# Twelve chunks of ada_w in layer 0's qkv stage: multiplied and summed by partition on VectorE instead of on TensorE

## The reference, cut to what matters

```python
silu_c = jax.nn.silu(c)            # c: (1, 1024)
silu_cc = jax.nn.silu(c_ctx)       # c_ctx: (1024,)
for i in range(DEPTH):             # DEPTH = 2
    mod_l = (silu_c @ ada_w[i] + ada_b[i])[:, None, :]
    mod_c = (silu_cc @ ada_w[i] + ada_b[i])[None, None, :]
    sh1_l, sc1_l, g1_l, sh2_l, sc2_l, g2_l = jnp.split(mod_l, N_MOD, axis=-1)
    ...
    a_l = ada_norm(h, norm_mix[i], sh1_l, sc1_l)          # needs sh1, sc1
    y_l, y_c = neighbourhood_attention_mixer(a_l, a_c, na_w_qkv[slot], ...)
    h = h + g1_l * y_l                                    # needs g1
    h = h + g2_l * swiglu_ffn(ada_norm(h, norm_ffn[i], sh2_l, sc2_l), ...)
```

## Time and profile before

| quantity | value |
|---|---|
| median of three runs | 1595.96 us (1595.84 to 1598.35) |
| profiled execution, its own time | 1595.65 us |
| its span in the trace | 1594.3 us |
| mean granted TensorE clock | 0.995 of full |
| TensorE busy | 1553.4 us, 97% |
| VectorE busy | 909.5 us, 57% |
| ScalarE busy | 688.3 us, 43% |
| GpSimd busy | 67.3 us, 4% |
| data moved by DMA | 251.19 MB, 158 GB/s on average |

### The profile page before, as it was taken

One profiled execution on the slowest core, in us unless ns is written; L12 is line 12 of the kernel. 1 busy time (PEld: TensorE's weight loads), 2 busy tenths in 40 slices (PEclk: granted clock), 3 DMA queues, 4 the chain that ended last, 5 costly groups with the idle time before them and its releaser, 6 DMA issues.

```text
span 1594.3 us, 25726 instructions
## 1 busy us (share of the span) xinstructions
PE 1553.4 (97%) x11195; PEld 1381.7 (87%) x11195; DVE 909.5 (57%) x1184; ACT 688.3 (43%) x932; POOL 67.3 (4%) x92
## 2 busy tenths in 40 slices
PE   5999999999999999999999999999999999999998
PEld 4778866867888888878778999999999999999998
DVE  5322488453432443357866555568777655677763
ACT  4311487332312321235764444545545446554552
POOL 2010031000000000000000000034000000000000
PEclk8999999999999999999999999999999999999999
DMA  9764421745433222364134555565555555555551
GB/s 327 246 205 159 139 35 21 264 160 184 159 106 106 93 92 85 101 230 141 54 122 144 185 185 172 180 213 183 173 184 180 184 179 164 165 175 185 179 174 71
DMA packets 254240, 251.19 MB, mean 158 GB/s; under 512 B 17085, under 2 KB 252960, under 8 KB 254128
## 3 DMA queue, kind: packets, MB, share of 16 engines
q1 hardware_dynamic: 252880, 247.48, 48.0%
q0 software_dynamic: 928, 1.94, 0.3%
q10 hardware_dynamic: 320, 0.13, 0.0%
HBM read 248.49 MB, written 1.05 MB: 157 GB/s over the span
## 4 chain that ended last, share of the span: by engine, by line
PE 88%; DVE 4%; ACT 2%; POOL 2%; issue 1%; DMA 1%; SPq 1%; DVEq 0%; ACTq 0%; POOLq 0%
PE psum L362 86%; PE psum L869 2%; DMA pre<-in_ada_w 1%; DVE sums L932 1%; POOL ptmp L1766 1%; DVE pt L946 1%; ACT wh L341 1%; DVE wl L348 1%; SPq L290 0%; DMA raw<-in_ada_w 0%; POOL ptmp L1765 0%; ACT scr L899 0%; DVE acc L1545 0%; POOL scr L1773 0%; ACT xh L632 0%
## 5 line engine op out<-in xcount | busy, mean ns | idle before, releaser
L362 PE MATMUL psum<-xh,wh 128*128 128x256 f32 (+1 forms) x1936 | 614.8, 318 | 5.0 <-DVE xl L676 2.8
L362 PE MATMUL psum<-xl,wh 128*128 128x256 f32 (+1 forms) x1936 | 608.5, 314 | 0.0
L362 PE MATMUL psum<-xh,wl 128*128 128x256 f32 (+1 forms) x1936 | 608.1, 314 | 0.0
L348 DVE TENSOR_TENSOR wl<-raw,wh 128x2048 fp32r<-128x2048 f32 (+1 forms) x186 | 418.4, 2250 | 275.2 <-ACT wh L341 275.0
L341 ACT ACTIVATE wh<-raw 128x2048 fp32r<-128x2048 f32 (+1 forms) x186 | 348.2, 1874 | 390.9 <-PE psum L362 384.9
L362 PEld LDWEIGHTS psum<-xh,wh 128*128 128x128 f32 x1936 | 369.5, 191 | 38.0 <-issue 9.8
L362 PEld LDWEIGHTS psum<-xh,wl 128*128 128x128 f32 x1936 | 369.6, 191 | 22.4
L362 PEld LDWEIGHTS psum<-xl,wh 128*128 128x128 f32 x1936 | 369.7, 191 | 21.8 <-issue 0.7
L362 PE MATMUL psum<-ah,wh 128*128 128x256 f32 (+1 forms) x704 | 217.9, 310 | 0.0
L362 PE MATMUL psum<-al,wh 128*128 128x256 f32 (+1 forms) x704 | 217.9, 310 | 0.0
L362 PE MATMUL psum<-ah,wl 128*128 128x256 f32 (+1 forms) x704 | 217.9, 309 | 0.0
(11 more groups left out here) (258 smaller groups left out, 1568.8 us busy)
## 6 DMA issues: line engine op xcount, KB each, us to landing
raw<-in_ffn_w_in SPq DMA_DIRECT2D x44, 1024.0 KB, 4.9
raw<-in_ada_w SPq DMA_DIRECT2D x25, 1024.0 KB, 5.3
pre<-in_ada_w SPq DMA_DIRECT2D x23, 1024.0 KB, 10.1
raw<-in_w_ffn_gate SPq DMA_DIRECT2D x22, 1024.0 KB, 5.1
raw<-in_w_ffn_up SPq DMA_DIRECT2D x22, 1024.0 KB, 5.2
raw<-in_ffn_w_out SPq DMA_DIRECT2D x16, 1024.0 KB, 5.1
raw<-in_w_ffn_down SPq DMA_DIRECT2D x16, 1024.0 KB, 4.9
raw<-in_na_w_qkv SPq DMA_DIRECT2D x12, 1024.0 KB, 6.0
```

Source lines behind the costliest of these rows:

```text
L348: dve.e.tensor_tensor(wl[:, c % NSPL, 0:z], raw[:, p % NRAW, 0:z], wh[:, c % NSPL, 0:z].bitcast(F32), ALU.subtract).then_inc(W.lo, 1)
L362: return pe.e.matmul(o, l, r, start=start, stop=stop, skip_group_check=shared)
```

## The change

In numbers of this kernel, ada_w chunks 8 to 19 (PARTS) are no longer matmuls. VectorE takes each loaded chunk and, for each of its k-tiles and for both condition vectors, multiplies by the column of silu(c) or silu(c_ctx) and adds into a tile of 128 partitions by 512 columns in `scr` (`ada_part`): 8 instructions per chunk. To have 512 columns, the chunks are cut differently: two neighbouring chunks of 8 k-tiles by 256 columns become one of k-tiles 0 to 3 by 512 columns and one of k-tiles 4 to 7 by 512 columns. Each is still 1 MB, with rows of 2 KB in DRAM instead of 1 KB. After every second such chunk TensorE adds over the partitions (`ada_sums`): four float32 matmuls of 256 columns with a stationary operand that has a column of ones, which stands in `adas` between zeros. So there are six of those, after weight chunks 3, 4, 6, 8, 10 and 11 (PART_SUMS).

The table `after`, which orders the loads, changes too: chunks 10 and 11 both follow weight chunk 4 in the list, and chunk 19 comes with weight chunk 12. A ring slot that held such a chunk is free when VectorE has done its eighth instruction. ScalarE waits for the last `ada_sums` before the attention, since `scr` is reused. Four semaphores of layer 1 are replaced by others that count on (K1.hi, K1.lo, R1.hi and R1.lo become J0.hi, J0.lo, B.hi and B.lo with offsets KH = 16 and QH = 8); the waits are the same.

```diff
-        after = {i: [8 + i] for i in range(12)}
+        after = {i: [8 + i + (i > 2)] for i in range(11)}
+        after[2] = [10, 11]
+
+        PARTS = range(8, 20)
+        PART_SUMS = {3: 0, 4: 1, 6: 2, 8: 3, 10: 4, 11: 5}
...
         def ada_src(a):
             l, i = ADA[a]
+            if a in PARTS:
+                half = (a - 8) % 2
+                return cols(ins["ada_w"][l], 256 * (i - half), 4 * half, 4, 512)
             return cols(ins["ada_w"][l], 256 * i)
...
                     kind_before, before = dma[p - NRAW]
-                    if kind_before == "ada":
+                    if kind_before == "ada" and before in PARTS:
+                        sp.wait_ge(A.part, 8 * (before - 8) + 8)
+                    elif kind_before == "ada":
                         sp.wait_ge(A.used, before + 1)
...
+        def ada_part(a):
+
+            b, half, p = (a - 8) // 2, (a - 8) % 2, pos["ada", a]
+            w = view(raw, p % NRAW, ada_src(a))
+            dve.wait_ge(s_raw[p % NRAW], 16 * (p // NRAW + 1))
+            dve.wait_ge(C.act, 1)
+            if b >= 3:
+                dve.wait_ge(A.used, 8 + 2 * (b - 2))
+            for k in range(4):
+                for s in range(2):
+                    to, c = scr[:, 2 * (b % 3) + s, :], sc[:, 8 * s + 4 * half + k:8 * s + 4 * half + k + 1]
+                    if half == 0 and k == 0:
+                        done = dve.e.tensor_scalar(to, w[:, k, :], c, None, ALU.mult)
+                    else:
+                        dve.wait_ge(A.part, 8 * (a - 8) + 2 * k + s - 1)
+                        done = dve.e.scalar_tensor_tensor(to, w[:, k, :], c, to, ALU.mult, ALU.add)
+                    done.then_inc(A.part, 1)
+
+        def ada_sums(b):
+
+            pe.wait_ge(C.dve, 5)
+            pe.wait_ge(A.part, 16 * b + 16)
+            pe.wait_ge(A.mod, ADA_FREE[LATE])
+            for half in range(2):
+                for s in range(2):
+                    j, row = 2 * half + s, 4 * b + 2 * half + s
+                    last = mm(ada_bank(LATE)[32 * j:32 * j + 32, 0:256], adas[:, 30 - row:62 - row],
+                              scr[:, 2 * (b % 3) + s, 256 * half:256 * half + 256], b == 0, b == 5)
+            last.then_inc(A.used, 2)
+
         def ada_pe(c):
+            if c in PART_SUMS:
+                ada_sums(PART_SUMS[c])
             for a in after.get(c, ()):
-                ada_mm(a)
+                if a not in PARTS:
+                    ada_mm(a)
...
             dve.e.tensor_scalar(gain[:, 0:1], gain[:, 0:1], 0.125, None, ALU.mult).then_inc(C.dve, 1)
+            dve.wait_ge(A.folded, 2)
+            dve.e.memset(adas[:, 0:62], 0.0).then_inc(C.dve, 1)
+            dve.wait_ge(C.dve, 4)
+            dve.e.memset(adas[:, 30:31], 1.0).then_inc(C.dve, 1)
...
                 if i == 1:
                     rest_dve()
+                for a in after.get(c - 1, ()):
+                    ada_part(a)
                 if i < 4:
                     continue
...
             bias_act(0)
+            act.wait_ge(A.used, 20)
             attention_act(C0, prep0(split_pair_hi, bias_act))
```

More of the change, by code:

```diff
@@ L406, in nothing @@
             pass
-        A = semaphores(nc, "ada", "used copied folded mod")
+        A = semaphores(nc, "ada", "used copied folded mod part")
         def ada_bank(b):
@@ L1241, in ffn0_dve @@
             diag_dve(2, 4)
-        K1 = semaphores(nc, "k1", "square copy stat root wide spread rot cos sum ctx hi lo")
-        R1 = semaphores(nc, "q1", "square copy stat rot cos sum hi lo root recip")
+        K1 = semaphores(nc, "k1", "square copy stat root wide spread rot cos sum ctx")
+        R1 = semaphores(nc, "q1", "square copy stat rot cos sum root recip")
+        KH, QH = 16, 8
         V1 = semaphores(nc, "v1", "half a d")
@@ L1324, in query_first @@
                 if i == 3:
-                    act.wait_ge(R1.lo, 1)
+                    act.wait_ge(B.lo, QH + 1)
                 act.e.activation(slot(q_sq[i]), qbank[i][:, :], ACT.Square).then_inc(R1.square, 1)
@@ L1330, in query_hi @@
                 act.wait_ge(R1.sum, i + 1)
-                act.e.activation(qh2[:, 2 * i:2 * i + 2, :], two(slot(q_sq[i])), ACT.Copy).then_inc(R1.hi, 1)
+                act.e.activation(qh2[:, 2 * i:2 * i + 2, :], two(slot(q_sq[i])), ACT.Copy).then_inc(B.hi, 1)
             split_for(split_hi, c_qkv1[0])
@@ L1357, in qkv1_act @@
                             act.wait_ge(K1.ctx, 4 * m + 2 * kv + 2)
-                            act.e.activation(kh2[:, 2 * m + kv, :], slot(k_out[m][kv]), ACT.Copy).then_inc(K1.hi, 1)
+                            act.e.activation(kh2[:, 2 * m + kv, :], slot(k_out[m][kv]), ACT.Copy).then_inc(J0.hi, 1)
                 if i >= 2:
@@ L1389, in query_lo @@
             def query_lo(i):
-                dve.wait_ge(R1.hi, i + 1)
+                dve.wait_ge(B.hi, QH + i + 1)
                 dve.e.tensor_tensor(ql2[:, 2 * i:2 * i + 2, :], two(slot(q_sq[i])), qh2[:, 2 * i:2 * i + 2, :].bitcast(F32),
-                                    ALU.subtract).then_inc(R1.lo, 1)
+                                    ALU.subtract).then_inc(B.lo, 1)
             split_for(split_lo, c_qkv1[0])
@@ L1430, in qkv1_dve @@
                         for kv in range(2):
-                            dve.wait_ge(K1.hi, 2 * m + kv + 1)
+                            dve.wait_ge(J0.hi, KH + 2 * m + kv + 1)
                             dve.e.tensor_tensor(kl2[:, 2 * m + kv, :], slot(k_out[m][kv]), kh2[:, 2 * m + kv, :].bitcast(F32),
-                                                ALU.subtract).then_inc(K1.lo, 1)
+                                                ALU.subtract).then_inc(J0.lo, 1)
                 if i >= 2:
@@ L1458, in score1 @@
             p, t = i // 2, i % 2
-            pe.wait_ge(K1.lo, p // 2 + 1)
-            pe.wait_ge(R1.lo, p // 2 + 1)
+            pe.wait_ge(J0.lo, KH + p // 2 + 1)
+            pe.wait_ge(B.lo, QH + p // 2 + 1)
             for n, (x, y) in enumerate(((qh2, kh2), (qh2, kl2), (ql2, kh2))):
```

## The result

The changed kernel takes 1632.63 us (median of four runs, 1632.37 to 1633.7), beside 1596.99 us for the kernel before in the same sessions (1595.84 to 1598.35): a ratio of 1.023 with a 95% interval of 1.0217 to 1.0243. The forecast was 1626.5 us with a range of 1617 to 1637; the measured time lies inside that range and 0.6 us above the forecast's own narrower range of 1621 to 1632. The profiled execution took 1633.7 us, with a span of 1632.3; that of before had 1594.3, so 38.0 us are to be found in the two traces.

What follows compares the result with a forecast made beforehand. TensorE set the pace before; the change makes a closed loop of load, splits and part the pace. Loop 29.4 + bias loads 0.5 + clock 1.0 = 30.9 us on 1595.65 gives 1626.5 us, range 1617 to 1637.

Steps and rivals of the forecast that it cites:

- The closed loop: Qkv stage: load 4.9, ScalarE split 1.95, VectorE split 2.32, part 4.9 in series, 14.1 us a step.
- TensorE's work: Qkv stage: twelve chunks off save 14.5 us, six sums of 0.79 add 4.7, so 9.8 us less work.
- Start of the chain: Qkv stage: part 8, the first on VectorE, runs from 61.2 to 66.1 us.
- The loads: Qkv stage: w4 to w13 each take 4.9 us once the part before is done; w5 2.7 us more.
- Rival 4: Qkv stage: loads issued together share the engines and both take 7.2 us, 1650 us in all; 5%.
- The products: VectorE's 128x512 instructions in the qkv stage: 0.60 us apart, 0.68 alone, 4.9 us a chunk, 59 us for twelve.
- Bias loads: SyncE's queue in the qkv stage: w8 delayed behind the bias loads by at worst 1.9 us, taken as 0.5.
- Start of the attention: After the qkv stage: steps follow as before and ScalarE's new wait ends with the same sum, nothing added.
- The clock: Dips in the qkv stage cost nothing; the attention starting at 1.2 GHz costs 1.0 us, bounds 0 and 4.
- rival 1: Qkv stage: loads and parts stay beside TensorE, -9.8 us, 1586 us, 3%; part about 2.5 us, within 0.2%, 2%.
- Rival 2: VectorE's parts slower: own-semaphore waits prevent overlap, 0.79 us each, 6.2 us a part, 1642 us; 9%.
- Rival 3: VectorE's parts faster: tensor_scalars at half their column time or cheaper SBUF operands, 1621 to 1623 us; 15%.

Runs made afterwards that it cites:

- products first: Changed kernel with VectorE's products of an ada chunk put before the split of weight chunk c + 2, from step 2 on: 1590.31 us, ratio 0.9957.
- the exp table early: One constant-column exp added before ScalarE's wait for the last sum: 1630.51 us in the changed kernel's order, 1587.79 us with products first.
- the same work without the tie: Kernel before plus the same 96 VectorE instructions reading a constant tile, so no load waits for them: 1598.87 us, ratio 1.0016.
- two and with four of eight: Changed kernel making only two or four of each ada chunk's eight products: 1589.11 us (ratio 0.9951) with two, 1602.36 us (1.0042) with four.

## Why the prediction was right, step by step

**The closed loop: right.** It is what cost the time. The new order of VectorE's list alone brings the loss (products first takes it away with everything else kept), and the rounds shown above run through load, two splits and part, as forecast. The terms follow, in the order of the prediction.

**TensorE's work: right.** A sum has 8 records (0.64 us, from 81.95); the second matmul behind it starts at 82.86, 0.78 us later than without it. The forecast was 0.79, and 9.8 us over the stage, which the kernel with the products first shows as 9.75. TensorE's last group ended at 203.4 (forecast near 199).

**Start of the chain: right.** Part 8 starts at 61.13 (forecast 61.2).

**The loads: right.** Nine of the ten landed within 4.73 to 4.99 us of their issue (4.9), that of w5 after 7.3, and ada chunks issued 0.46 us behind a weight chunk did not hold it up. Rival 4 falls.

**The products: mis-sized, in both directions.** All products by form in the changed kernel (count, busy us, mean ns):

```profile
L458 DVE SCALAR_TENSOR_TENSOR scr<-raw,small,scr 128x512 f32<-128x512 f32 x84 | 58.0, 762 | 0.0
...
L455 DVE TENSOR_SCALAR scr<-raw,small 128x512 f32<-128x512 f32 x12 | 5.3, 482 | 0.0
```

A row of eight scalar_tensor_tensors takes 5.39 us, so one starts every (5.39 - 0.74) / 7 = 0.66 us and not 0.60; my nearest row had one operand in PSUM. A tensor_scalar of 512 columns starts 0.40 us after the one before and lasts 482 ns, not 0.60 and 681. The Trainium skill (VectorE: DVE Perf Modes, "The perf-mode tier table") has tensor_scalar on fp32 in SBUF at two elements a cycle, a rule that I set aside because L685 with 256 columns took 0.32 us. By that page's clock of 0.96 GHz, an estimate for 512 columns is 0.27 us at two a cycle and 0.53 at one. The measured 0.40 is below 0.53, so for this form the trace agrees with the page. What differs in L685 is two column operands and two operations instead of one; no run here tells which of them matters.

Parts are thus 4.86 and 5.39 us by turns instead of 4.9. Part 13 took 6.81 us, while GpSimd masked the attention bias next to it: its masks ran from 128.45 on and took 1.0 to 1.2 us each beside the part, 0.74 alone. In the kernel with the products first the masks met part 14, and it was part 14 that was slow. All twelve are 62.8 us instead of 58.8. VectorE's split hands over 0.1 us sooner than I had it, ten times, and part 19 ends at 217.54 instead of 214.4.

**Bias loads: smaller.** w8 landed after 4.96 us; I had set 0.5 us for it and it cost nothing. The bias cost 1.4 us at another place, by the masks beside part 13, which the forecast did not have.

**Start of the attention: a step was missing.** I had priced ScalarE's new wait at nothing ("ends with the same sum"). It does end with it, but the order on ScalarE shows that the table load had taken over a wait:

```order
62 L765 ACTIVATE bias_h<-bias 128x768 [waits bias_masked]
63 L947 ACT_TABLE_LOAD [waits att_max]
64 L947 ACTIVATE scr,sums<-psum,sums 128x256 [waits ada_used]
```

With one wait in front of the exp, that wait stood on the exp and the table load was free; with two, one of them stands on the table load. That was to be read from the order before the forecast. It cost 1.3 us (forecast 0). With it removed (the exp table early, in the change's order), the attention still loses 0.75 us beside the copy of `adas`. That is what is left for the clock (forecast 1.0), which was at half until 226.2 us there and until 227.9 in the change; that the clock is the whole cause of it is argued and not shown.

**The clock: right in the stage, and incomplete behind it.** TensorE's granted clock (third last column, 1.00 for 2.4 GHz and 0.50 for 1.2) in the changed kernel while it idled, at the first scores, and in matmuls of layer 1 and of the second block:

```profile
210.00:211.00 1.00, 0.00 (x0) 0.00 (x0) 1.00 (x1) 1.00 (x3) 0.00 (x0) 0.50 0.22 75
218.00:219.00 1.00, 0.68 (x8) 0.00 (x0) 0.40 (x2) 0.00 (x0) 0.00 (x0) 0.50 0.44 86
...
226.00:227.00 1.00, 1.00 (x6) 0.67 (x6) 1.00 (x2) 0.16 (x1) 0.00 (x0) 0.50 0.00 0
228.00:229.00 1.00, 1.00 (x9) 0.86 (x8) 0.08 (x1) 0.77 (x4) 0.00 (x0) 1.00 0.00 0
771.00:773.00 2.00, 2.00 (x12) 2.00 (x11) 0.23 (x1) 2.00 (x3) 0.00 (x0) 0.50 1.07 380
1095.00:1097.00 2.00, 2.00 (x11) 2.00 (x11) 1.57 (x4) 1.90 (x2) 1.09 (x1) 0.50 0.44 100
```

In the stage the half-rate stretches cost only 0.4 us, in the last sum (1.08 us instead of 0.64), as TensorE was not on the chain before it. The last two rows are the remaining 3.0 us of the 38.0: at 771 and 1095 us the clock went to 1.2 GHz for 3.4 us each, in code that the change does not touch, and the shift grew by 1.5 us each time. Just before each of them TensorE had a row of very narrow matmuls, of 2 columns and of 1:

```profile
768.30 1.93 PE L371 MATMUL psum<-cst,hs_t 128*128 128x2 f32 x16
...
1092.55 1.02 PE L371 MATMUL psum<-cst,acc 128*128 128x1 f32 x8 [0.91 <-DVE acc L1599]
```

These are two fixed places of the program. Of the eight profiles, five have a half-rate stretch at the first place (the change 770.6, products first 729.4, the same work without the tie 737.7, and both kernels with the exp table early, 725.8 and 769.0), and three at the second (the change and both with the table early). Every one of them starts 1.8 to 3.0 us after the first of the narrow matmuls. The profile of before has the same matmuls at 733.3 and 1056.0 and neither stretch, like those with two and with four of eight. So the stretch comes in some executions and not in others, but not anywhere; that the narrow matmuls cause it is not shown. The medians, 35.6 us apart, seem to carry fewer of them than the two profiles. What the forecast stood for is 33.0 us up to the copy of `adas` and 2.0 at the start of the attention, 35.0 us against a forecast 30.9.

**Rivals.** The gain of 9.8 us (rival 1) came true in another order, by cutting the loop rather than by shorter products; its threshold of 2.1 us a part was roughly right: with 0.9 or 1.4 us a part the change gains, with 2.1 or 2.7 it loses. Its other half, a part of about 2.5 us ending within 0.2% of before, was too narrow: with 2.4 on average the kernel is 0.4% slower. Rival 2, 0.79 us each (the row it is taken from gives 0.80), is excluded by 0.66. Rival 3 was right in its mechanism, the faster tensor_scalars, and outweighed by the slower other form.

## What to carry to other kernels

When a buffer of a ring is handed to another engine, write down who frees it, what stands in front of that instruction in its engine's list, and who loads what that one waits for: if the way leads back to the same ring, the loads can no longer run ahead, and once the sum of the loop is longer than the step of the busiest engine, that sum is the step, however idle the engines are. (With two products the loop was there too, but shorter than TensorE's step, and the kernel gained.) Where the loop exists, look for two neighbouring items in one list whose exchange cuts it, here the products before the split. And after adding a wait, read from the order on which instruction it has come to stand.

## What the runs showed of the hardware that was not expected

- scalar_tensor_tensor of 128x512 float32 with two SBUF tensors runs every 0.66 us, with one of them in PSUM every 0.60 us (L1269, 684 ns alone, against 745 ns). Whether the second operand is the chunk just loaded or a constant makes no difference: eight take 5.39 us in both.
- tensor_scalar of 128x512 float32, SBUF to SBUF with one column operand: 482 ns, 0.40 us apart.
- Where GpSimd's masks ran beside such products, both took longer: eight products 6.81 us instead of 5.39 in the change and 9.20 in the same work without the tie, single ones up to 1227 ns instead of 745, and the masks 1.0 to 1.2 us instead of 0.74.
- TensorE's clock can go to half for 3.4 us in the middle of its work, at about 1.5 us each, in some executions of a program and not in others. Between 240 us and the last 15 us of the eight profiles this happened at two places only, each just behind a row of matmuls of 1 or 2 columns. The kernel before spreads over 1594.35 to 1599.07 us in 15 runs, and the mean granted clock falls from 0.996 in its fastest to 0.991 in its slowest.
